# Block one's up-projections with the tokens stationary: pairs of weight groups stream 512 columns wide through TensorE, and VectorE and ScalarE turn the products back

## The reference, cut to what matters

```
def swiglu(h, w_gu, w_down):
    gate, up = jnp.split(h @ w_gu, 2, axis=-1)
    return (jax.nn.silu(gate) * up) @ w_down

for l in range(DEPTH):                                  # DEPTH = 2
    x = x + 0.5 * swiglu(rmsnorm(x, ffn1_norm[l]), ffn1_w_gu[l], ffn1_w_down[l])
    x = x + hybrid_mixer(...)
    x = x + 0.5 * swiglu(rmsnorm(x, ffn2_norm[l]), ffn2_w_gu[l], ffn2_w_down[l])
```

## Time and profile before

| | |
|---|---|
| median of 3 runs | 2634.85 us (2634.54 to 2636.7) |
| the profiled execution | 2637.17 us |
| its span in the trace | 2635.4 us |
| PE busy | 2597.9 us, 99% |
| DVE, ACT busy | 1412.5 us (54%), 528.1 us (20%) |
| mean rate of all DMA | 157 GB/s |

### The profile page before, as it was taken

One profiled execution on the slowest core, in us unless ns is written; L12 is line 12 of the kernel. 1 busy time (PEld: TensorE's weight loads), 2 busy tenths in 40 slices (PEclk: granted clock), 3 DMA queues, 4 the chain that ended last, 5 costly groups with the idle time before them and its releaser, 6 DMA issues.

```text
span 2635.4 us, 51104 instructions
## 1 busy us (share of the span) xinstructions
PE 2597.9 (99%) x21966; PEld 2358.8 (90%) x21966; DVE 1412.5 (54%) x2409; ACT 528.1 (20%) x1121; POOL 7.3 (0%) x17
## 2 busy tenths in 40 slices
PE   8999999999999999999999999999999999999999
PEld 8999777889999999877888999869996799967999
DVE  6674254315766766244331766346672566535665
ACT  2111132111111111123210111331113411133110
POOL 0000000000000000000000000000000000000000
PEclk9999999999999999999999999999999999999999
DMA  6664322146555555421125556423444144431443
GB/s 264 222 220 180 120 84 78 65 159 219 199 213 220 195 221 209 160 101 68 57 105 208 214 218 225 172 92 133 163 174 159 45 158 176 173 128 65 160 161 113
DMA packets 52529, 414.98 MB, mean 157 GB/s; under 512 B 4080, under 2 KB 6384, under 8 KB 32080
## 3 DMA queue, kind: packets, MB, share of 16 engines
q1 hardware_dynamic: 48256, 357.96, 37.0%
q10 hardware_dynamic: 3456, 50.33, 5.2%
q0 software_dynamic: 592, 3.41, 0.3%
HBM read 410.64 MB, written 1.05 MB: 156 GB/s over the span
## 4 chain that ended last, share of the span: by engine, by line
PE 95%; DVE 2%; ACT 1%; DMA 1%; DVEq 1%; issue 0%; ACTq 0%; SPq 0%
PE units L820 31%; PE spots L820 23%; PE units L745 14%; PE units L941 7%; PE spots L1131 2%; PE units L1242 2%; PE spots L801 2%; PE units L1289 2%; PE units L1407 1%; PE units L919 1%; PE units L912 1%; DMA context_keys<-cond 1%; PE spots L1338 1%; PE spots L1319 1%; PE spots L1328 1%; ACT probabilities L1476 1%
## 5 line engine op out<-in xcount | busy, mean ns | idle before, releaser
L820 PE MATMUL units<-normed,weights 128*128 128x128 f32 x2176 | 270.5, 278 | 13.5 <-DMA weights<-stream 8.6
L820 PEld LDWEIGHTS units<-normed,weights 128*128 128x128 f32 x2176 | 257.3, 194 | 17.1 <-issue 16.8
L820 PE MATMUL spots<-normed,weights 128*128 128x128 f32 x2176 | 265.7, 275 | 0.2
L820 PEld LDWEIGHTS spots<-normed,weights 128*128 128x128 f32 x2176 | 254.3, 192 | 0.6 <-ACT normed L1476 0.3
L745 PE MATMUL units<-normed,weights 128*128 128x256 f32 x1040 | 230.6, 382 | 2.2 <-ACT normed L1476 2.2
L745 PEld LDWEIGHTS units<-normed,weights 128*128 128x128 f32 x1040 | 197.9, 191 | 32.4 <-issue 5.9
L1476 ACT ACTIVATE mla_q_rope<-units 128x256 f32<-128x256 f32 (+1 forms) x248 | 95.3, 387 | 529.1 <-PE units L820 488.3
L941 PE MATMUL units<-normed,weights 128*128 128x256 f32 x832 | 193.6, 387 | 0.0
L2106 DVE TENSOR_TENSOR delta_new_values<-spots,mla_q_rope 128x256 f32<-128x256 f32 x116 | 49.2, 424 | 266.0 <-PE spots L820 266.0
L941 PEld LDWEIGHTS units<-normed,weights 128*128 128x128 f32 x832 | 155.7, 191 | 29.3 <-issue 8.0
L820 PE MATMUL units<-hidden,weights 128*128 128x128 f32 x1472 | 180.9, 276 | 0.0
(11 more groups left out here) (371 smaller groups left out, 3535.1 us busy)
## 6 DMA issues: line engine op xcount, KB each, us to landing
weights<-stream SPq DMA_DIRECT2D x138, 2048.0 KB, 7.8
weights<-stream SPq DMA_DIRECT2D x48, 1024.0 KB, 5.2
values_mla_qk_mla_values<-stream ACTq DMA_DIRECT2D x24, 2048.0 KB, 8.0
weights<-stream SPq DMA_DIRECT2D x16, 768.0 KB, 6.4
constants<-consts SPq DMA_DIRECT2D x1, 1094.5 KB, 16.5
residual<-x_in SPq DMA_DIRECT2D x1, 1024.0 KB, 4.8
weights<-stream SPq DMA_DIRECT2D x4, 256.0 KB, 5.3
conv_in<-ctx_in POOLq DMA_DIRECT2D x1, 1024.0 KB, 8.5
```

The lines of the kernel that those rows point to most:

```text
L820: mm = pe.matmul(dst[:, m * P:m * P + P], weights[:, m, kt, :], moving(kt), start=(first and m == 0 and kt == 0), stop=(kt == n - 1), skip ...
```

## The change: what it does

1. **Units.** Two weight groups make one up unit. A feed-forward part has 5 wide units and one of a single group (6 up units, `FFN_UP`), then 6 down units as before.
2. **Products.** In the up units the 128 tokens of a half are the stationary operand and the weights are moving, 512 columns wide (256 in the single unit): 4 matmuls for a product. The seven products and PE's order of them stay. The results have tokens on the partitions.
3. **Scale and gate.** `rstd` is turned once per part into a column for each token half (`token_rstd`); ACT applies it as the scale of its silu, which reads the sum directly, and DVE multiplies in one instruction per half.
4. **Back to feature-major.** DVE transposes within 32x32 blocks (two instructions of 128x512), and ACT puts the blocks in place: 16 copies of 32x256 per wide unit (`move_blocks`), between its keeping of `u4` and of the next unit's `c1`. The differences of unit k-1 are made within unit k (`differences`).
5. **Slots.** `vqv` becomes a fourth slot for the feed-forward parts, and a table (`FFN_SLOTS`) gives the slots. A wide unit takes two; they are loaded when P3 of the unit before the previous one has ended. The down groups 0 and 1 go where wide unit 4 was.
6. **Ada.** Its weights go to free tiles in two loads of 1 MB; units `ADA_FIRST` = 1, 2, 3, 5, 7, 9 and `ADA_AT` = 1, 2, 3, 4, 6, 8 (of 12). None is in the last unit, number 11.
7. **Opening.** The first product waits for the first halves of two groups, the second for two whole groups.

```
-ADA_AT = (1, 4, 7, 10, 13, 16)
-ADA_FIRST = (3, 5, 8, 10, 13, 16)
+ADA_AT = (1, 2, 3, 4, 6, 8)
+ADA_FIRST = (1, 2, 3, 5, 7, 9)
...
+FFN_SLOTS = ([0, 1, 2, 3] * 2 + [0, 1, 2] + [0, 1, 2] * 2, [2, 3, 0, 1] * 2 + [2, 3, 0] + [2, 3, 1, 2, 3, 2])
...
+                def freed(c, n):
...
+                    which = int(n >= FFN2_BASE)
+                    return p3_done.at(c, FFN_MU * which + ffn_unit(n - MU_GROUP["one"][which]) + 1)
...
+                    if rows_:
+                        out_ = dst.rearrange("p (g c) -> p g c", c=T)
+                        for kt in range(n):
+                            w = weights[kt // 2][:, :, kt % 2] if type(weights) is list else weights[:, :, kt]
+                            mm = pe.matmul(out_, moving(kt), w, start=(first and kt == 0), stop=(kt == n - 1),
+                                           skip_group_check=True)
+                        return mm
...
+                def move_blocks(k):
+
+                    n = mu_width(c, k)
+                    e_.wait_ge(*h_made.at(c, up * which + k + 1))
+                    src = h_turned[:, :, 0:n].rearrange("p t (m b i) -> p b t m i", b=4, i=32)
+                    dst = hT[:, 4 * k:4 * k + n // P, :].rearrange("p m (t a i) -> p a t m i", t=TT, i=32)
+                    for a in range(4):
+                        for b in range(4):
+                            ins = activate(dst[32 * b:32 * b + 32, a], src[32 * a:32 * a + 32, b], ACT.Copy)
+                    ins.then_inc(h_moved.handle, 1)
...
+                    ve.wait_ge(*u4_kept.at(c, base + k + 1))
+                    ve.wait_ge(*p7_done.at(c, base + k + 1))
+                    ve.tensor_tensor(wide_c2[1][:, 0:n], v_bank[:, 0:n], kept_u4(c, k), ALU.add).then_inc(c22_made.handle, 1)
+                    early_sums(c, which, k + 1)
+                    sum_two(k + 1)
+                    if k:
+                        differences(k - 1)
+
+                    sum_four(k + 1)
+                    ve.wait_ge(*u2_kept.at(c, base + k + 1))
+                    ve.wait_ge(*p4_done.at(c, base + k + 1))
+                    ve.tensor_tensor(wide_c2[0][:, 0:n], v_bank[:, 0:n], kept_u2(c, k), ALU.add).then_inc(c21_made.handle, 1)
+                    ve.drain()
+                    for t in range(TT):
+                        ve.wait_ge(*gate_made.at(c, 2 * (up * which + k) + 1 + t))
+                        ins = ve.scalar_tensor_tensor(h_tok[t][:, 0:n], wide_c2[t][:, 0:n], token_rstd[:, t:t + 1], h_tok[t][:, 0:n],
+                                                      ALU.mult, ALU.mult)
+                    ins.then_inc(x_taken.handle, 1)
+                    ve.drain()
+                    for t in range(TT):
+                        ins = ve.transpose(h_turned[:, t, 0:n], h_tok[t][:, 0:n])
+                    ins.then_inc(h_made.handle, 1)
```

More of the change, by code:

```diff
@@ L299, in signal @@
             return Signal(sem(name), counts, first)
-        slot = [sb(f"weights{s}", [P, FULL]) for s in range(SLOTS)]
+        weights = sb("weights", [P, SLOTS + 1, FULL])
+        slot = [weights[:, s, :] for s in range(SLOTS + 1)]
         xT = sb("residual", [P, KD, T])
@@ L619, in load_small, with load @@
                     sp.dma_start(bias_a, bada).then_inc(bias_here, 16)
-                def load(n, start, wait):
-                    (name, i), w, here = list(GROUP[sec])[n], slot[n % SLOTS], loaded[n % SLOTS]
+                def load(c, n, start, wait):
+                    (name, i), w, here = list(GROUP[sec])[n], slot[SLOT_OF[sec][n]], loaded[SLOT_OF[sec][n]]
                     sp.wait_ge(*wait)
+                    if sec == "one" and n == FFN2_BASE + 1:
+                        sp.wait_ge(*merged_made.at(c, 4))
                     if name == "down":
@@ L839, in raw @@
                     if k >= up:
-                        units = DOWN_HALF if c.sec == "one" else (2,) * 4
+                        units = (2,) * (3 if c.sec == "one" else 4)
                         chunk = (k - up) % len(units)
@@ L1522, in load_ada @@
                 places_, size = STREAM["one"]
-                e_.dma_start(vqv[:, :], stream[bass.ds(c.turn * size + places_["ada", i], P * FULL)].rearrange(
-                    "(p w) -> p w", p=P)).then_inc(ada_loaded.handle, 16)
+                rows_ = stream[bass.ds(c.turn * size + places_["ada", i], P * FULL)].rearrange("(p h w) -> p h w", p=P, h=2)
+                for half in range(2):
+                    e_.dma_start(ada_w[half], rows_[:, half, :]).then_inc(ada_loaded.handle, 16)
             def multiply(c, which):
@@ L2123, in multiply @@
-                        if k == up + downs and c.sec != "two":
-                            add_four(c, (2 * which) if first else 1)
-                            if first and which == 0:
-                                gained(mix_in, V_MIX, range(4))
-                            elif next_layer:
-                                ve.wait_ge(*vec_here.at(next_layer, 16))
-                                gained(act, V_FFN1, range(4))
-                                ve.drain()
-                                first_difference()
```

382 lines of the change are left out of this document (241 added, 141 removed).

## The result

The changed kernel takes 2655.18 us (median of 4 runs, 2654.21 to 2656.31), the kernel before 2634.69 us beside it. The ratio is 1.0077, with a 95% interval of 1.006 to 1.0095: 20.5 us slower. The prediction said 2638 and at most 2653. The profiled execution took 2656.31 us, its span is 2654.5 against 2635.4 before, 19.1 us more (the profiled executions lie 1.1 and 2.5 us above these medians).

A forecast was written before the change was run, and what follows sets the result against it. PE was taken as the bound, busy 2597.9 of 2635.4 us. A saving of 21.2 us met about 24 us of new waits, summing to +2.9 us and 2638 us, with a range of 2627 to 2653.

The forecast's parts named there:

- the saving on PE: Up units: twenty wide units save 1.01 us each and four single units 0.26 us each, -21.2 us.
- loads of wide units 2, 3, 4: PE waits before P1 for 4 MB loads, 0.53 us in each of 12 units, +6.4 us.
- down unit 0: Its load follows P3 of wide unit 4; waits of 0.67 and 2.75 us, twice each, +6.8 us.
- down unit 5, second part: Its load follows P3 of down 3, three products ahead of P1; 1.4 us, twice, +2.9 us.
- last unit without ada: P4 waits for P5's result with no ada piece over that chain; 1.1 us at four ends, +4.4 us.
- layer 1's first unit: Four early sums delay the normed tiles; P2 waits 1.8 us instead of 0.25, +1.6 us.
- opening: First loads and sums put P6 of unit 1 at 47.0 us, 0.5 us later than before; +1.8 us.
- thin place at down unit 1: VectorE makes the single unit's differences ahead of the third sum P6 needs; +1.0 us (0 to 6).
- given back: P6 of the second part no longer waits for a weight sum, -0.8 us.
- Together 0.2 + 7.8 + 4.9 = 12.9 us, a wait of 0.53 us: Wide-unit pair loads: issue delay, first 2 MB load and second load, against a window of 12.37 us before P1.
- the loads bind harder: Rival: a second load adds 5.9 us, so the twelve P1 waits are 18 us, 2650 us; chance 0.25.
- The way back to feature-major: Wide units: copies free up to 0.88 us each; rival at 1 us, waits of 1 to 2 us, 2670; chance 0.07.

The follow-up runs named there:

- run 9: Changed kernel with halved pair loads, new down slots, VectorE work moved, last ada piece in unit 11, another in unit 5, constants one unit earlier still: 2616.44 us.
- Run 1: Changed kernel with the loads of wide units 2, 3, 4 cut in halves, both first halves issued first: 2642.89 us, ratio 1.0028.
- Run 2: Changed kernel with another slot table for the down groups, so loads for down units 0 and 5 get slots that come free earlier: 2643.36 us.
- Run 3: Changed kernel with rotary angles and constants moved to wide units 2, 3, 4 and the single unit's differences behind the third sum: 2652.16 us.
- run 6: Changed kernel with halved loads, new slots, VectorE and ada moves, and ScalarE's 16 copies replaced by one that misplaces blocks: 2617.15 us.
- Run 7: Changed kernel with halved loads, new slots, VectorE and ada moves, and ScalarE's 16 copies made twice: 2702.29 us, ratio 1.0253.
- run 8: Kernel before the change, with only the last ada piece of each feed-forward part moved from unit 16 to 15: 2640.0 us, ratio 1.0016.
- run 4: Changed kernel with the last ada piece of each feed-forward part back in the last unit, 11: 2646.54 us, ratio 1.0045.

## Why the prediction was wrong, step by step

The sum ended at +2.9 us, the span grew by 19.1. Each wait below is the gap to the work ahead of it in the trace of the changed kernel.

| step of the prediction | foreseen | trace after |
|---|---|---|
| the saving on PE | -21.2 | see below |
| loads of wide units 2, 3, 4 | +6.4 | +14.6 |
| down unit 0 | +6.8 | +8.3 |
| down unit 5, second part | +2.9 | +3.7 |
| last unit without ada | +4.4 | +4.4 |
| layer 1's first unit | +1.6 | +1.0 |
| opening (P6 of unit 1 at 47.25, not 47.0) | +1.8 | +2.0 |
| thin place at down unit 1 | +1.0 | +2.2 |
| given back | -0.8 | -0.8 |
| rotary work and constants on VectorE | not in the sum | +2.7 |
| lower clock behind two waits | not in the sum | +3.5 |
| mixers | not in the sum | -1.7 |

With -21.2 the right column ends at +18.7, and 19.1 was measured. That is 15.8 us above the sum of the prediction, and over half of it, 8.2, is the row of the pair loads.

- **The saving was right.** A wide product is 3.43 us (1500.10 to 1503.53). With the new waits taken out, the four feed-forward parts of run 9 are 19.1 us shorter than before (3.5, 5.4, 4.8 and 5.4); the foreseen -21.2, +1.8 for the opening and -0.8 given back make 20.2. By the medians run 9 is 18.0 us faster. By the spans it is 20.7, but 1.6 of that lie behind the feed-forward parts, where the change does nothing; a lower clock that the kernel before has there, at 2313 us, has no counterpart in run 9.
- **The step that failed: "Together 0.2 + 7.8 + 4.9 = 12.9 us, a wait of 0.53 us".** The mechanism was right: PE waits at P1 for the second load of the pair. The size was not: 14.6 us in place of 6.4. The window was 12.23 us and not 12.37 (12 x 0.14 = 1.7 us). The landing was 12.03 us plus the wait after the issue: in the six units of layer 0 12.76 on the average (12.5 to 13.3) against 12.7 foreseen, in the six of layer 1 13.74 (12.5 to 14.3). So the two-load price of the earlier trace rows held in layer 0, and the rival's, 5.9 us for the second load, in layer 1; why they differ stays open. The Trainium skill (DMA: Bandwidth & Descriptors, Where 436 GB/s comes from) lets about 358 GB/s bind between HBM and SBUF; an estimate from it is 5.9 us for the second load and 13.7 for the pair. The average of layer 1 agrees with it, layer 0 does not. Run 1 shows that these waits were the loads' price, and that nothing else in the wide unit stood ready to replace them.
- **Down units 0 and 5 (12.0 instead of 9.7 us)** waited for single loads. In layer 0's second part these landed 8.9 us (771.22 - 762.33) and 7.8 us (837.36 - 829.60) after the issue, where 7.8 and 6.6 were reckoned. SP had issued more loads right behind each; that these were the reason is not shown. Run 2 removes the waits.
- **The rival "the loads bind harder" was the nearest**, with 18 us of waits and 2650. It was short because the terms around it were short as well: the range took its upper end from one term at its bound and left all others at their middle.
- **VectorE at the rotary work (+2.7) was overlooked.** The prediction counted VectorE's time for a wide unit and for down unit 0, and not what else the program puts into units 6 and 7 (`ROTARY_AT` is `FFN_UP`, and that moved with the change). Run 3 removes it.
- **The lower clock (+3.5) was not in the sum.** In the kernel before PE has no wait over 0.3 us in the feed-forward parts after the opening, so its trace could not show it there. It could be read elsewhere in that trace, though the page's slices, 66 us each, all show a clock of 90% or more. Outside these parts PE pauses four times for 2.2 to 2.4 us, and three of the pauses are followed by windows of 4 us at 0.59 to 0.74. One of them, a product that takes 1.95 us at full clock, with its window:

```profile
2428.51 3.66 PE L820 MATMUL units<-normed,weights 128*128 128x128 f32 x16 [2.21 <-ACT normed L1476]
...
2428.00:2432.00 4.00, 3.48 (x17) 3.48 (x18) 3.42 (x9) 3.27 (x8) 0.00 (x0) 0.60 0.55 233
```

- **The mixers (-1.7) do not belong to the change's idea.** In layer 1's mixer of the kernel before a pause of 2.4 us, for which the profile names no releaser, is followed by a product of 5.4 us instead of 3.6. After the change the pause there is 0.8 us and the clock stays up, which makes the -3.3. The +1.6 in layer 0's mixer is such a pause too (1.66 us). In each of the two longer ones a packet of the queue for instructions lands; that PE waits for it is likely, and no run shows it.
- **The way back to feature-major was judged rightly in the wide units.** A copy takes 0.413 us against 0.411 assumed, and by run 6 the 16 copies cost the program about 1 us more than one copy would. Run 7 bounds the reckoned room: at twice the copies wide units still wait nothing. The prediction named one thin place, down unit 0 to down unit 1; with twice the copies there are three, from the single unit to down unit 1.
- **Ada**: the traces of run 8 in the kernel before and of run 4 in the changed one give the 4.4 us of the four gaps.

## What to carry to other kernels

When an edit halves the number of units in flight, the load's window shrinks with it. Before anything else, list for each load the work between its issue and its first reader; split it by what the first reader needs (here P1 needs half, and that alone gave 12 us). Work that seems to lie idle in the order, as the ada piece in the last unit, may be a cover: price it by what starts late without it. And when small waits are summed for an engine that had none, add the price of the clock, and let the range take several terms at their bounds at once.

## What was not expected of the hardware

- **The lower clock behind a wait is not certain.** The changed kernel and runs 1 to 4 have, after the opening, fifteen waits of PE of 2.0 to 4.0 us in the feed-forward parts; ten were followed by windows of 4 us with a clock of 0.58 to 0.90, five by none. Down unit 0's wait of 3.9 us at 771.22 kept full clock, one of 2.0 us in run 2 did not. A fall costs 1.7 to 1.8 us. The Trainium skill (TensorE: Matmul & The Clock Gate, HAM oscillation — how this bites in real kernels) describes a kernel with waits of about 3 to 5 us for transfers, whose clock falls at every one. Of the three waits here that are that long (3.6 to 3.9 us, down unit 0 in the changed kernel and in runs 3 and 4) two were followed by a fall, and eight shorter ones were too.
- **Pairs that met a code fetch landed later.** The DMA view of the changed kernel over a pair in layer 0 (660 to 673 us), and one in layer 1 (1501 to 1515 us), where a 16 KB packet of the queue for instructions lies inside:

```profile
q1 hardware_dynamic: 288, 4.19, 80.5%
...
q1 hardware_dynamic: 288, 4.19, 76.0%
q8 instruction: 1, 0.02, 0.4%
```

The six pairs of layer 0 meet no such packet of queue q8. All six of layer 1 have one in their stretch, and five of them land 13.7 to 14.3 us after the issue; the sixth, where it comes as the last bytes land, 12.5. Runs 2 to 4, which keep these loads, repeat it: their 18 pairs of layer 0 meet no such packet and wait 0.4 to 1.3 us, their 18 of layer 1 all meet one, and 14 of them wait 1.6 to 2.1 us, four only 0.5 to 0.7. That P1 waits of over 1.3 us come only with such a packet is shown; that the fetch is the cause is not, since every one of these pairs is in layer 1, and no run moved the code. Why layer 1 has a fetch there and layer 0 none is open too.
